# TensorE's loop over the pairs of the two feed-forward stages, written out as straight code

## What is computed

```
def swiglu(h, wg, wu, wd):
    return (jax.nn.silu(h @ wg) * (h @ wu)) @ wd

for i in range(DEPTH):                       # DEPTH = 2
    h = rmsnorm(x, norm_mix_w[i])
    ...                                      # layer 0: retention and gated delta; layer 1: Mamba-2 state space
    x = x + out
    x = x + swiglu(rmsnorm(x, norm_ffn_w[i]), ffn_w_gate[i], ffn_w_up[i], ffn_w_down[i])
y = rmsnorm(x, norm_final_w)
```

## Time and profile before

| | |
|---|---|
| median of 3 runs | 3728.67 us (3727.29, 3728.67, 3735.23) |
| own time of the profiled execution | 3735.23 us |
| its span, first to last instruction | 3735.3 us |
| TensorE busy | 3305.7 us, 88% |
| VectorE, GpSimd, ScalarE busy | 1671.6, 1206.6, 727.5 us |
| mean granted TensorE clock | 0.933 of full speed |

### The profile page before, as it was taken

How to read it: one execution, slowest core, us unless ns; L and a number is a source line. 1 busy time by engine, 2 the same in 40 slices (tenths; PEclk the granted TensorE clock), 3 DMA queues, 4 the chain that set the end, 5 groups by cost and what they waited for, 6 DMA issues and landing times.

```text
span 3735.3 us, 50309 instructions
## 1 busy us (share of the span) xinstructions
PE 3305.7 (88%) x20042; PEld 3153.2 (84%) x20042; DVE 1671.6 (45%) x1828; ACT 727.5 (19%) x1062; POOL 1206.6 (32%) x528
## 2 busy tenths in 40 slices
PE   6999787797869999999958897998988799999997
PEld 6888777697759999999958696896977699999996
DVE  5334546464551232222366757567476422223224
ACT  3202323132230000000133314223133200000001
POOL 2222211021013343333313444444344233333431
PEclk9999898798979999999979899998999899999998
DMA  3111100001001111111113213122132011111111
GB/s 137 58 58 52 38 24 23 25 29 35 13 23 51 46 46 46 46 46 46 40 28 83 74 57 96 49 73 84 53 90 63 29 51 46 46 46 46 47 49 59
DMA packets 103687, 191.38 MB, mean 51 GB/s; under 512 B 20948, under 2 KB 63348, under 8 KB 103320
## 3 DMA queue, kind: packets, MB, share of 16 engines
q1 hardware_dynamic: 47200, 145.80, 11.6%
q10 hardware_dynamic: 56248, 42.11, 4.3%
HBM read 164.07 MB, written 19.59 MB: 49 GB/s over the span
## 4 chain that ended last, share of the span: by engine, by line
PE 79%; issue 8%; DVE 8%; ACT 2%; DMA 1%; POOL 1%; DVEq 0%; ACTq 0%; SPq 0%; POOLq 0%
PE ps_set L458 65%; ACT work L916 2%; PE ps_core L858 2%; PE ps_core L705 1%; PE ps_core L723 1%; DMA work<-ssm_cum_rows 1%; PE ps_set L495 1%; PE ps_core L853 1%; PE ps_core L863 1%; DVE work L1741 1%; DVE work L1306 0%; PE ps_core L654 0%; DMA w_raw<-in_w 0%; PE ps_core L714 0%; PE ps_core L779 0%
## 5 line engine op out<-in xcount | busy, mean ns | idle before, releaser
L382 POOL TENSOR_TENSOR w_hi<-w_raw,small 128x1024 fp32r<-128x1024 f32 x230 | 448.2, 1949 | 2253.6 <-PE ps_set L458 2237.0
L458 PE MATMUL ps_set<-h_hi,w_hi 128*128 128x344 f32 x3888 | 868.0, 332 | 89.8 <-DVE h_lo L1317 34.6
L458 PE MATMUL ps_set<-h_lo,w_hi 128*128 128x344 f32 x3888 | 838.4, 324 | 0.0
L458 PE MATMUL ps_set<-h_hi,w_lo 128*128 128x344 f32 x3888 | 832.2, 323 | 0.0
L458 PEld LDWEIGHTS ps_set<-h_hi,w_hi 128*128 128x128 f32 x3888 | 667.6, 192 | 114.3 <-issue 101.7
L458 PEld LDWEIGHTS ps_set<-h_lo,w_hi 128*128 128x128 f32 x3888 | 671.0, 193 | 10.2 <-issue 10.2
L458 PEld LDWEIGHTS ps_set<-h_hi,w_lo 128*128 128x128 f32 x3888 | 659.7, 191 | 0.0
L385 POOL TENSOR_TENSOR w_lo<-w_raw,w_hi 128x1024 fp32r<-128x1024 f32 x230 | 610.3, 2654 | 18.0
L1623 DVE TENSOR_TENSOR work<-work,ps_set 128x1032 f32<-128x1032 f32 x44 | 54.1, 1229 | 829.8 <-PE ps_set L458 829.8
L458 PE MATMUL ps_set<-y_hi,w_hi 128*128 128x344 f32 x1440 | 319.0, 331 | 35.0 <-DVE y_lo L1610 17.7
L1341 DVE TENSOR_TENSOR x<-x,ps_set 128x1032 f32<-128x1032 f32 x176 | 216.3, 1229 | 275.1 <-PE ps_set L458 275.1
(11 more groups left out here) (204 smaller groups left out, 3172.9 us busy)
## 6 DMA issues: line engine op xcount, KB each, us to landing
w_raw<-in_w SPq DMA_DIRECT2D x230, 512.0 KB, 3.3
work<-ssm_cum_rows ACTq DMA_DIRECT2D x32, 512.0 KB, 8.9
sample<-in_ssm_state SPq DMA_DIRECT2D x16, 512.0 KB, 4.2
out_ssm_s<-sample SPq DMA_DIRECT2D x16, 512.0 KB, 3.1
x<-in_x SPq DMA_DIRECT2D x8, 516.0 KB, 8.6
work<-work ACTq DMA_DIRECT2D x16, 258.0 KB, 2.4
out_y<-x ACTq DMA_DIRECT2D x8, 516.0 KB, 3.0
sample<-bc_rows SPq DMA_DIRECT2D x8, 512.0 KB, 4.8
```

Source lines behind the costliest of these rows:

```text
L382: return nc.gpsimd.tensor_tensor(w_hi[:, k, :], w_raw[:, k, :], zeros, ALU.add)
L458: mm = nc.tensor.matmul(out[:, g, 0:TN], w[:, slot, cols], v[:, g * TN:(g + 1) * TN], start=(start and n == 0), stop=(stop and n == 2))
```

## The change

The loop at L807 becomes a loop of Python, so the program contains the five turns one after the other. All waits that used registers become waits for constants. This happens in both feed-forward stages, since they share the function. The loops of the other engines, and TensorE's loops in the other stages, stay.

```diff
                 for k, job in ((2, "gb"), (3, "ub")):
                     tile(first, job, 0, base + k, base + k)
-                with pe.Fori(0, (PAIRS - 1) // 2) as i:
+                for i in range((PAIRS - 1) // 2):
                     for k in range(2):
                         unit = i * 12 + (base + 4 + 6 * k)
                         tile(loop, f"ga.{k}", i, unit, base)
```

## The result

The changed kernel takes 3713.80 us in the median of six runs (3700.52 to 3718.88), against 3734.15 us (3727.29 to 3742.99) for the kernel before, which ran three more times beside it. The ratio is 0.9942, with a 95% interval of 0.9924 to 0.9960: 0.6% faster. The forecast of 3705.0 against the 3728.67 known then is a ratio of 0.9937, well inside the interval. The profiled execution of the changed kernel took 3715.04 us, its span is 3713.2 us.

A forecast was written before the change was run, and what follows sets the result against it. TensorE, busy 88% of the span, was taken to bound the kernel. Savings of 19.63 us in feed-forward 0 and 4.09 us in feed-forward 1, together 23.7 us off the median, gave 3705.0 us, range 3699 to 3718.

The forecast's parts named there:

- TensorE is the path, and gaps go straight into the time: Feed-forward stages: TensorE busy 197 to 199 of 200 us, so each of its gaps adds directly to the end time.
- The sum: Both feed-forward stages: 19.63 us saved in feed-forward 0 and 4.09 us in feed-forward 1, 23.7 us together.
- Slow matmuls behind the gaps: Feed-forward 0: matmuls slowed by lower clock after gaps, with the pipeline emptying, cost 6.0 us that goes too.
- Registers, waits, the other engines: 0: Feed-forward stages: dropped register instructions, constant waits and engines that wait for TensorE change the time by 0 us.
- Fetching straight code: 0: TensorE's instruction queue in the feed-forward stages: packets of straight code arrive in time, costing 0 us.
- The rival of starvation: Feed-forward stages: each new packet of straight code makes TensorE wait, at most 2.33 us, up to 3868 us; chance 0.05.
- The moved state-space edge: State-space loop's way back, at a new address: its 1.17 us gap may change by -0.2 to +2.2 us; taken as 0.
- It removes eight taken branches, and with them the gaps: TensorE's feed-forward loops: four branches a stage go, with their 13.6 and 4.1 us of gaps and slow matmuls behind.
- the paragraph on blocks: State-space edge: code comes in 16 KiB blocks of 256 instructions; a branch outside what is held stalls until its block arrives.
- the rival of gaps alone: Feed-forward gaps go, but slow matmuls stay and the state-space edge worsens: 15.5 us saved, 3711 to 3718 us; chance 0.12.
- the likeliest one: Feed-forward stages: both gaps and slow stretches go, giving 3705 us, range 3699 to 3711; chance 0.75.

The follow-up runs named there:

- run 7: Changed kernel with all remaining loops of all engines (TensorE, VectorE, ScalarE, GpSimd, SyncE) also written out; ratio 0.9910 to the kernel before, median 3695.65 us.
- run 3: Kernel before, loops kept, with 40 already-held waits (20 instructions) ahead of norm 1, moving feed-forward 0's loop; ratio 0.9956.
- run 8: Kernel before, loops kept, with 138 already-held waits (69 instructions) ahead of norm 3, moving feed-forward 1's loop; one profiled execution, 3750.34 us.
- run 9: Kernel before, both loops kept, with 40 already-held waits ahead of norm 1 and 152 ahead of norm 3; ratio 0.9939, median 3718.90 us.
- Run 1: Kernel before with only feed-forward 0 made straight code, feed-forward 1 keeping its loop; ratio 0.9946.
- run 2: Kernel before with only feed-forward 1 made straight code, feed-forward 0 keeping its loop; ratio 0.9980.
- run 4: Kernel before, loops kept, with 386 already-held waits (193 instructions) ahead of norm 3, moving feed-forward 1's loop; ratio 1.0005.
- run 5: Kernel before with TensorE's feed-forward loops making ten turns of one pair instead of five of two; ratio 0.9916, median 3705.92 us.

## Why the prediction was right, and where its reason was wrong

**TensorE is the path, and gaps go straight into the time.** Right. The two stages lost 25.7 us in the profile.

**The sum.** 23.7 us were forecast, 19.6 and 4.1; 20.6 and 5.1 were measured. The term is short by 1.0 us in each stage. I took 136.57 us for a turn without gap, but a piece that ends at a gap contains the emptying of the pipeline; in the unbroken piece four turns take 706.0 - 160.7 = 545.3 us, 136.3 each. The two matmuls between two gaps show the same: 0.57 us, 0.25 more than 2 x 0.158.

**Slow matmuls behind the gaps.** Stages without gap show none inside: 706.0 us in nearly all of them, 707.3 once (run 7). Only their first microseconds, behind the waits ahead of the stage, are partly at the lower level. After the change the first 19 us have a granted clock of 0.92 in both stages and the rest has 1.00; in run 7 the first 19.4 us have 0.84, and its 1.3 us lie there. That the gap of 3 to 4 us is the cause in feed-forward 0 agrees with run 3, where it went with the gap, and with run 8, where two gaps of about 1 us with 11 matmuls between left the clock at 1.00. Why the first two double gaps, of 3.1 us each, were followed by clocks of 0.78 and 1.00 stays open.

**Registers, waits, the other engines: 0.** Right. Runs 3 and 9 keep registers and branches and reach the same 706 us.

**Fetching straight code: 0.** Right. 4464 matmuls crossed 36 packets in feed-forward 0 and 35 in feed-forward 1 without a gap. The rival of starvation is out.

**The moved state-space edge.** I took 0 and gave -0.2 to +2.2 us; it was +1.3 us, a second gap, as the count of its place had made possible. Run 1, which moves it as the change does, and runs 3 and 9, which move it by 20 instructions, have the second gap too (1.60, 1.54 and 1.27 us); runs 2, 4 and 8, which don't move it, have one.

**The step that fails is the sentence "It removes eight taken branches, and with them the gaps".** The gaps went and the size came out right, but the branch is only half of the reason. Runs 3, 5 and 9 keep the branches, in run 5 nine a stage for four, and have no gap. Fetching isn't the reason alone either: straight code fetches 36 and 35 packets a stage and has no gap. What costs is both together, a way back to code that TensorE no longer holds. Then 9 packets come a turn, and TensorE stands until 2.2 to 3.1 us after the first of them has started. I had read this row and used it only to show that straight code asks for no more, and I had named the condition in the paragraph on blocks without pricing anything by it. A loop that is kept was not among the rivals. So the forecast was right for this kernel at this address, and that the address was a costly one was luck: with 20 instructions more ahead of feed-forward 0, as in run 3, the change would have had only the 5.1 us of feed-forward 1 to win.

A turn of 1761 instructions (864 matmuls with their weight loads, and 33 others) was fetched anew at one address and kept at another one 20 instructions further on; one of 882 was kept in both stages. The turn of feed-forward 1 has 1754 instructions and stood at six addresses: it was fetched anew with one gap at four (before, and moved in runs 1, 3 and 4), with two gaps at one (run 8), and kept at one (run 9). How many gaps a refetched turn has depends on where its head stands: just ahead of a packet's end, two (feed-forward 0 before, run 8); at the other four addresses, one.

The Trainium skill ("Runtime: NRT & Kernel Launch", Instruction fetch mechanics) gives TensorE a memory of 128 KiB, 2048 instructions, filled in blocks of 256. By it I would expect a turn of 1761 to fit if it touches seven blocks, while one that touches all eight leaves no room for the block that is fetched ahead; this would be why 20 instructions decide. That is an estimate, and the runs agree with it, but I tried no third address for the loop of feed-forward 0. The page goes on that prefetch is purely sequential, that there is no instruction cache that benefits from spatial locality, and that a taken branch out of a window of two pages forces a fetch. There the measurements differ: 1761 instructions are nearly seven blocks of 256, and run 3 executed them four more times without a packet. Runs 3, 5 and 9 fetched 36, 80 and 71 packets fewer than the kernel before, while their traces have 20, 35 and 96 instructions more.

**The distance to the forecast.** 3705 was forecast from a median of 3728.67 of three runs; with six runs it is 3734.15. The difference measured is 20.4 us against 23.7, and the scatter ahead of feed-forward 0 covers that. Taken by itself, 3713.80 us lies in the range that the prediction gave to the rival of gaps alone, 3711 to 3718, and not in the likeliest one, 3699 to 3711. The lengths of the stages decide against that rival: the slow matmuls went too, and it is the median of the kernel before that came out 5.5 us higher.

**What stays open.** Why the stretch before feed-forward 0 varies by 16 us with the same code; which loop gave run 7 its gain, and how much; and whether the count of blocks is the exact rule for what is kept.

## What to carry to other kernels

Before a loop is written out, count what its turn fetches: if the instruction queue moves a whole turn's packets each turn, look for a gap at each way back. On TensorE there was one in both feed-forward stages, and a shorter turn (here half as long) cured it as well as straight code did, with less code. Where another wait ends later, as in retention, the gap is worth little. Where no packets moved, straight code gained nothing over the loop (706.05 us in both). And a change that makes code longer or shorter moves every loop behind it, which here made from nothing to 3.4 us of gaps an edge (13.6 us in four) by address alone; compare lengths of stages, not only totals, before such a difference is credited to the edit.

## What the runs showed of the hardware that I had not expected

- A loop of 1761 instructions on TensorE needed 9 instruction packets a turn at one address, and none at an address 20 instructions on: 184 packets and 726.7 us, against 148 and 706.05.
- With the code at hand, four or nine taken branches a stage cost nothing that can be seen: 706.05 and 706.03 us, against 706.05 for straight code.
- The gap of a refetched turn in a feed-forward stage was 0.7 to 1.2 us where there was one. A second one added 2.1 to 2.7 us where it stood two matmuls behind the first, and 0.7 to 1.3 us where it stood 11 matmuls behind.
- At each of these gaps TensorE went on 2.2 to 3.1 us after an instruction packet had started, while straight code crossed 36 and 35 such packets a stage without a gap.
